# SSM preparation of a hybrid backbone: exponents by 34-row one-pass products plus a mask product, an exponential per direction, nothing computed on POOL

## The chip, the cores and the metric

One core of one Trainium2 chip runs the whole program. The metric is the device time of one execution in microseconds (us), the median of several runs. Engines: PE (TensorE; PEld are its weight loads), DVE (VectorE), ACT (ScalarE), POOL (GpSimd), SP (SyncE). A letter q behind an engine (SPq, POOLq) means its queue: what it issues or waits for.

## The reference, cut to what matters

Two layers of a backbone with three token mixers. The third is a bidirectional Mamba-2 state-space scan (SSD) over chunks of tokens. The preparation computes, for every tile of 128 tokens and each of 16 heads, the part of the output that stays inside the tile. Per direction:

```
acum  = cumsum(a)                                    # a = dt * A, the log decay, per token and head
lmat  = exp(where(lower, acum[l] - acum[s], -inf))   # 128 x 128 per head; the mirror image for backward
cb    = C[l] . B[s]                                  # 128 x 128 per group of 8 heads
y     = (cb * lmat) @ (x * dt)                       # 64 channels per head
out   = y_forward + y_backward + ssm_d * x
```

There are 1024 sample tokens and 128 prompt tokens, so 9 tiles per layer (NT = 9), 16 heads (SH), 64 channels per head (SP_), 2 groups (SG).

## The kernel before

Each layer is a sequence of phases with a barrier of all five engines between them. After the projections (phase 1) comes the decay phase (phase 2): DVE and ACT compute dt and the log decay `logd` of all tiles, PE sums them to `cum` (running sums, times triangles of ones) and `tot`, and a few rows are turned and stored in DRAM (`cumrow_d`, `betarow_d`, L691 and L692) before the barrier. Then comes the stage in question, the SSM preparation (phase 3), followed by the SSM scan.

The preparation treats the 9 tiles one after another; tile t is double buffered by p = t % 2. For a tile:

- SP loads `xin` (12 blocks of 128x128, L698), and later stores the turned tokens `xt` (L702).
- PE turns 10 blocks (L1003) into PSUM banks 0 to 2 and makes the two group products `cb` in bank 7 (L1005). Then it makes the exponents of all 16 heads in banks 3 to 6: for each head one f32 product of `after` with a triangle of ones (forward, L1014) and one of `before` with the other triangle (backward, L1015), added in PSUM. Last it makes the 32 output products of the **previous** tile (two per head: L990 with `w_f`, L991 with `w_b`), 64 columns each, into banks 0 and 1.
- ACT copies the turned tile to `xt` (L1443) and takes the exponential in two halves of 8 heads (`e_ssm`, L1450).
- DVE masks `cb` by both triangles (L1991), builds `after` for the next tile (L1980: a strict triangle times the log decay, in two halves), adds the output products of the previous tile to `d_x` (`y_sum`, L1984, one instruction of 1024 elements), makes `x_dt[0]` (L2000), `d_x` (L2001) and `w_f` (L2004, two halves).
- POOL builds `before` (L1676), `x_dt[1]` (L1688) and `w_b` (L1692) in the same way.

PE's next turning (L1003 of tile t + 1) writes the banks that the output products of tile t - 1 were in, so it waits for `y_sum(t - 1)`:

```
if not (isinstance(t, int) and t < 2):
    pe.wait_ge(sp_yd, n - 1)
```

After the last tile PE waits for `y_sum(7)` and makes the output products of tile 8. The tiles 0, 1 and 8 are written out, 2 to 7 are a loop.

Of the kernel before, what the change touches and what calls it, by code (L numbers as in the profile page):

```python
# [24 lines left out]
ALU = mybir.AluOpType  # L25
# [5 lines left out]
P = 128  # L31
# [86 lines left out]
def backbone_kernel(nc, A, O, table, rope_table):  # L118
    with ExitStack() as ctx:
# [13 lines left out]
        ssm_tok_d = dram("ssm_tok_d", [NT, P, 1280])  # L133

# [56 lines left out]
        plus_half = fixed("plus_half", [P, GH])  # L191
        r_tok = fixed("r_tok", [P, NT])
# [37 lines left out]
        after = place(a, "after", [P, SH, P])  # L230
        before = place(a, "before", [P, SH, P])
        e_ssm = place(a, "e_ssm", [P, SH, P])
        w_f = place(a, "w_f", [P, SH, P])
        a2 = fresh(WT)
        w_b = place(a2, "w_b", [P, SH, P])
        x_dt = [place(a2, f"x_dt{n}", [P, SH, SP_]) for n in range(2)]
        d_x = place(a2, "d_x", [P, SH, SP_])
        cb = [place(a2, f"cb{n}", [P, 2, SG, P]) for n in range(2)]
# [108 lines left out]
        rest = place(a, "rest", [P, 2, NT, 20])  # L347
        cum_g = place(a, "cum_g", [P, NT, 2, GH])
# [53 lines left out]
        sp_prod = sem("sp_prod")  # L402
        sp_fwd = sem("sp_fwd")
        sp_bwd = sem("sp_bwd")
        sp_e = sem("sp_e")
        sp_yd = sem("sp_yd")
        sp_y = sem("sp_y")
# [242 lines left out]
        def _(sp):  # L650
# [14 lines left out]
            with sp.Fori(0, DEPTH) as l:  # L665
# [24 lines left out]
                sp.wait_ge(row_made, l + 1)  # L690
# [212 lines left out]
        def _(pe):  # L903
# [21 lines left out]
            with pe.Fori(0, DEPTH) as l:  # L925
# [53 lines left out]
                last.then_inc(decay_prod, 1)  # L979
                barrier(pe, l, 2)  # L980


                def y_products(n, late):

                    for half in range(2):
                        pe.wait_ge(sp_fwd, n * 6 + (5 + late + half))
                        pe.wait_ge(sp_bwd, n * 4 + (3 + late + half))
                        for h in range(8 * half, 8 * half + 8):
                            dst = PSUM[:, h * SP_:(h + 1) * SP_]
                            pe.matmul(dst, w_f[:, h], x_dt[0][:, h], start=True, stop=False)  # L990
                            last = pe.matmul(dst, w_b[:, h], x_dt[1][:, h], start=False, stop=True)  # L991
                    last.then_inc(sp_y, 1)

                def ssm_prep(t, p, i):
                    n = l * NT + t
                    first = isinstance(t, int) and t == 0
                    pe.wait_ge(tile_in[p], loaded(l, p, i, 0))
                    if not first:
                        pe.wait_ge(sp_fwd, n * 6 - 2)
                    if not (isinstance(t, int) and t < 2):  # L1000
                        pe.wait_ge(sp_yd, n - 1)
                    for k in range(10):
                        pe.transpose(PSUM[:, k * P:(k + 1) * P], xin[p][:, k], ident)  # L1003
# [3 lines left out]
                    for half in range(2):  # L1007
                        if not first:
                            pe.wait_ge(sp_e, n * 2 + (half - 1))
                        pe.wait_ge(sp_fwd, n * 6 + (1 if first else -1) + half)  # L1010
                        pe.wait_ge(sp_bwd, n * 4 + (1 if first else -1) + half)
                        for h in range(8 * half, 8 * half + 8):
                            dst = PSUM[:, 1536 + h * P:1536 + (h + 1) * P]
                            pe.matmul(dst, after[:, h], cst[:, C_TRI], start=True, stop=False)  # L1014
                            last = pe.matmul(dst, before[:, h], cst[:, C_TRI + 1], start=False, stop=True)  # L1015
                        last.then_inc(sp_prod, 1)
# [1350 lines left out]
```

## Time and profile before

| what | value |
|---|---|
| median of 3 runs | 5475.16 us (5473.5 to 5489.51) |
| the profiled execution: its own time / its span | 5479.28 us / 5477.5 us |
| granted TensorE clock, mean of the span | 0.865 of full |
| PE / PEld busy | 4459.5 us (81%) / 4161.0 us (76%) |
| DVE / ACT / POOL busy | 2261.2 us (41%) / 932.3 us (17%) / 798.0 us (15%) |
| SSM preparation, layer 1 | 1091.40 to 1284.59 us of the span (193.2 us) |
| SSM preparation, layer 2 | 3786.40 to 3980.26 us (193.9 us) |

The busy shares are of the whole program. The preparation is two stretches of about 193 us in it, and only these and the short decay phases ahead of them are changed. A granted clock of 1.00 is 2.4 GHz, one of 0.50 is 1.2 GHz.

### The profile page before, as it was taken

How to read it: one execution, taken by the hardware profiler on the slowest of the kernel's cores; microseconds unless marked ns; L12 is line 12 of the kernel's file. 1: busy time of each engine (PE TensorE's matmuls, PEld its weight loads, DVE VectorE, ACT ScalarE, POOL GpSimd, SP SyncE). 2: the span in 40 equal slices, each digit the busy share in tenths (PEclk: the TensorE clock that was granted, in tenths of full speed). 3: DMA queues.
4: the chain of work that ended last, by engine and by line, in shares of the span. 5: the costliest groups of instructions: out<-in, count | busy, mean ns of one | idle time of the engine just before them, and what ended most of it. 6: DMA issues, size and time to landing. Idle time of an engine off the chain costs nothing.

```text
span 5477.5 us, 67948 instructions
## 1 busy us (share of the span) xinstructions
PE 4459.5 (81%) x26457; PEld 4161.0 (76%) x26457; DVE 2261.2 (41%) x2622; ACT 932.3 (17%) x1477; POOL 798.0 (15%) x668
## 2 busy tenths in 40 slices
PE   5899999787794775798759999996878828649977
PEld 2899999784783665788739999996848728648867
DVE  2532511277425245544235143114863243464442
ACT  2111100010211220342021011001111112114410
POOL 0010000077110002100000000002660100030000
PEclk7999999898785777899879999997988658769988
DMA  6222222123234332001242222221142434310024
GB/s 207 96 88 78 89 95 86 48 85 116 84 108 157 113 104 78 8 8 59 96 165 86 83 82 94 94 78 55 63 142 77 141 121 126 100 51 7 8 76 149
DMA packets 418307, 492.97 MB, mean 90 GB/s; under 512 B 83102, under 2 KB 354512, under 8 KB 410612
## 3 DMA queue, kind: packets, MB, share of 16 engines
q1 hardware_dynamic: 385160, 392.54, 22.9%
q0 software_dynamic: 28240, 96.75, 4.6%
q8 instruction: 134, 2.20, 0.2%
q10 hardware_dynamic: 4700, 0.88, 0.1%
q14 instruction: 73, 0.60, 0.0%
HBM read 333.19 MB, written 156.91 MB: 89 GB/s over the span
## 4 chain that ended last, share of the span: by engine, by line
PE 70%; DVE 9%; DMA 8%; issue 4%; SPq 3%; POOL 2%; ACT 2%; DVEq 1%; POOLq 0%; ACTq 0%
PE PSUM L633 14%; PE PSUM L634 14%; PE PSUM L635 14%; PE PSUM L1271 5%; PE PSUM L1118 4%; PE PSUM L1292 3%; PE PSUM L991 1%; PE PSUM L990 1%; DMA g_XY<-xy_d 1%; PE PSUM L1260 1%; DMA w_mod<-in_w_mod 1%; SPq L823 1%; POOL x_in L1710 1%; PE PSUM L1261 1%; PE PSUM L1096 1%
## 5 line engine op out<-in xcount | busy, mean ns | idle before, releaser
L633 PE MATMUL PSUM<-h_hi,w_hi 128*128 128x384 f32 x3456 | 1156.5, 335 | 40.6 <-DVE w_lo L619 40.6
L635 PE MATMUL PSUM<-h_hi,w_lo 128*128 128x384 f32 x3456 | 1156.0, 334 | 0.0
L634 PE MATMUL PSUM<-h_lo,w_hi 128*128 128x384 f32 x3456 | 1156.0, 334 | 0.0
L633 PEld LDWEIGHTS PSUM<-h_hi,w_hi 128*128 128x128 f32 x3456 | 650.1, 188 | 40.7 <-issue 40.7
L634 PEld LDWEIGHTS PSUM<-h_lo,w_hi 128*128 128x128 f32 x3456 | 650.1, 188 | 0.0
L635 PEld LDWEIGHTS PSUM<-h_hi,w_lo 128*128 128x128 f32 x3456 | 649.9, 188 | 0.0
L633 PE MATMUL PSUM<-b_hi,w_hi 128*128 128x384 f32 x1152 | 394.6, 343 | 108.5 <-DVE w_lo L619 56.4
L617 DVE CAST w_hi<-w_raw 128x2048 fp32r<-128x2048 f32 (+1 forms) x104 | 118.9, 1144 | 789.1 <-PE PSUM L635 587.1
L634 PE MATMUL PSUM<-b_lo,w_hi 128*128 128x384 f32 x1152 | 391.9, 340 | 0.0
L635 PE MATMUL PSUM<-b_hi,w_lo 128*128 128x384 f32 x1152 | 391.4, 340 | 0.0
L1658 POOL DMA_DIRECT2D proj_d<-leave x140 | 82.5, 589 | 1744.7 <-ACT leave L1411 669.4
L633 PEld LDWEIGHTS PSUM<-b_hi,w_hi 128*128 128x128 f32 x1152 | 221.9, 193 | 113.9 <-issue 107.7
L2285 DVE TENSOR_REDUCE row_max<-PSUM 128x1 f32<-128x1152 f32 (+1 forms) x144 | 178.3, 1238 | 252.0 <-PE PSUM L1261 252.0
L1271 PE MATMUL PSUM<-v_all,prob_t 128*128 128x64 f32 x2336 | 278.1, 274 | 0.1
L1271 PEld LDWEIGHTS PSUM<-v_all,prob_t 128*128 128x128 f32 x2336 | 275.2, 194 | 0.5 <-DVE prob_t L2296 0.5
L1118 PE MATMUL PSUM<-g_XY,g_t 128*128 128x128 f32 x288 | 59.9, 393 | 251.2 <-DMA g_XY<-xy_d 243.7
L1118 PEld LDWEIGHTS PSUM<-g_XY,g_t 128*128 128x128 f32 x288 | 55.1, 293 | 254.2 <-DMA g_XY<-xy_d 202.4
L619 DVE TENSOR_TENSOR w_lo<-w_raw,w_hi 128x2048 fp32r<-128x2048 f32 (+1 forms) x104 | 221.3, 2128 | 7.9
L634 PEld LDWEIGHTS PSUM<-b_lo,w_hi 128*128 128x128 f32 x1152 | 222.1, 193 | 0.0
L635 PEld LDWEIGHTS PSUM<-b_hi,w_lo 128*128 128x128 f32 x1152 | 221.6, 192 | 0.0
L1411 ACT ACTIVATE leave<-PSUM 128x1152 f32<-128x1152 f32 x60 | 68.1, 1135 | 680.7 <-PE PSUM L635 680.7
L1292 PE MATMUL PSUM<-cst,prob 128*128 128x128 f32 x1168 | 157.9, 278 | 25.5 <-ACT prob L1598 25.4
(294 smaller groups left out, 7010.7 us busy)
## 6 DMA issues: line engine op xcount, KB each, us to landing
w_raw<-in_w_in SPq DMA_DIRECT2D x70, 1024.0 KB, 5.2
proj_d<-leave POOLq DMA_DIRECT2D x140, 512.0 KB, 2.9
g_t<-gdn_tile_d SPq DMA_DIRECT2D x36, 1024.0 KB, 8.6
gdn_tile_d<-g_out SPq DMA_DIRECT2D x18, 1792.0 KB, 7.0
wide<-proj_d SPq DMA_DIRECT2D x48, 576.0 KB, 3.8
w_mod<-in_w_mod SPq DMA_DIRECT2D x12, 2048.0 KB, 18.8
xs<-ssm_tok_d SPq DMA_DIRECT2D x36, 640.0 KB, 5.0
qk_t<-proj_d SPq DMA_DIRECT2D x36, 512.0 KB, 9.6
```

Of the source, the lines that this page charges most:

```text
L617: dve.tensor_copy(w_hi[p][:, 0:kt], w_raw[p][:, 0:kt])
L619: dve.tensor_tensor(w_lo[p][:, 0:kt], w_raw[p][:, 0:kt], w_hi[p][:, 0:kt].bitcast(F32), ALU.subtract).then_inc(w_ready[p], 1)
L633: pe.matmul(dst, wh, x_hi[:, k, lo:hi], start=(k == 0), stop=False)
L634: pe.matmul(dst, wh, x_lo[:, k, lo:hi], start=False, stop=False)
L635: last = pe.matmul(dst, wl, x_hi[:, k, lo:hi], start=False, stop=(k == kt - 1))
L823: sp.dma_start(gd[d]["XY"][t % 2][at, :, at], src.rearrange("h x (j i) -> j h x i", i=SOLVE)).then_inc(scan_in[d][t % 2], 16)
L1118: last = pe.matmul(bank(n, P, h * P), lhs(h), rhs(h), start=True, stop=True)
L1271: last = pe.matmul(bank(7, AD, h * AD), prob_t[s][:, j], v_all[:, kt, g * AD:(g + 1) * AD], start=(j == 0), stop=(j == len(key_tiles) - 1))
L1292: last = pe.transpose(dst, prob[s][:, j * P:(j + 1) * P], ident)
L1411: act.activation(thirds(leave[b][:, 0:T]), acc(b), f, scale=sc).then_inc(leave_ready[b], 1)
L1658: pool.dma_start(proj_d[j * 2 + (blk + b), :, 0:SAMPLE], leave[b][:, 0:SAMPLE]).then_inc(leave_out[b], 16)
L2285: dve.tensor_reduce(row_max[:, u, h:h + 1], PSUM[:, 1536 * (h % 2):1536 * (h % 2) + nk * P], AX_X, ALU.max, negate=True).then_inc(at_m, 1)
```

## The change

The exponents are no longer sums over triangles. The running sums `cum` exist already; the exponent of (s, l) is their difference. Each is split into a coarse part (rounded to fp32r, the one-pass format) and the rest (`ssm_hl`), turned by PE in the decay phase, and stored in DRAM as `ssmrow_d`. Per tile and direction POOL's queue loads 32 rows (`s_col`) and two long rows (`s_row[32:34]`) from there. One product over 34 rows, 4 heads wide (512 columns), gives the differences; a second one, the identity times a constant of 0 and -1e30 (`far_r`), adds the mask. The directions are now separate: own exponent products, own exponential, own weights `w_ssm[d]`. The output products stay as they are (32 f32 products of 64 columns), but are made in two groups of 8 heads, with the exponents of the second direction between them, and `y_sum` is done by halves. `d_x` moves from DVE to ACT as 16 activations of 64 columns, `x_dt[1]` and the backward weights move from POOL to DVE, `after` and `before` are gone, `cb` is copied unmasked. `x_dt` and `d_x` are double buffered. The loops over tiles are written out.

```
@@ tiles in SBUF
-        after = place(a, "after", [P, SH, P])
-        before = place(a, "before", [P, SH, P])
+        e_ssm = [place(a, f"e_ssm{d}", [P, SH, P]) for d in range(2)]
+        w_ssm = [place(a, f"w_ssm{d}", [P, SH, P]) for d in range(2)]
+        s_row = [place(a2, f"s_row{d}", [34, SH, P], F32R) for d in range(2)]
+        s_col = [place(a2, f"s_col{d}", [34, P], F32R) for d in range(2)]
+        x_dt = [[place(a2, f"x_dt{n}{d}", [P, SH, SP_]) for d in range(2)] for n in range(2)]
@@ decay phase: SP, PE, ACT, POOL, DVE
-                sp.wait_ge(row_out, l * 32 + 32)
+                sp.wait_ge(row_made, l * 2 + 2)
+                sp.dma_start(flat_rows[0:512].rearrange("(c p) n -> p c n", p=P), ssm_rows[:, 0:4].bitcast(F32)).then_inc(row_out, 16)
+                sp.dma_start(flat_rows[512:576], ssm_rows[0:64, 4].bitcast(F32)).then_inc(row_out, 16)
+                sp.wait_ge(row_out, l * 64 + 64)
+                for c in range(5):
+                    last = pe.transpose(bank(6, P, c * P)[0:width] if c < 4 else bank(7, P)[0:width], ssm_cols[:, c * P:c * P + width], ident)
+                act.activation(ssm_rows[:, 0:4], bank(6).rearrange("p (c n) -> p c n", n=P), ACT.Copy)
+                act.activation(ssm_rows[0:64, 4], bank(7, P)[0:64], ACT.Copy).then_inc(row_made, 1)
+                pool.tensor_tensor(head_of[:], ident[0:32, 0:SH], ident[0:32, SH:32], ALU.add)
+                for d in range(2):
+                    pool.tensor_scalar(s_row[d][0:32], over(head_of[:], P), -1.0, None, ALU.mult)
+                    pool.tensor_copy(s_col[d][32:34], ones[32:34])
+                    dve.tensor_copy(ssm_hl[:, :, d, 0], cum[:, d, :, 4:20])
+                dve.drain()
+                    dve.tensor_tensor(ssm_hl[:, :, d, 1], cum[:, d, :, 4:20], ssm_hl[:, :, d, 0].bitcast(F32), ALU.subtract)
@@ PE, preparation
+                def y_products(t, half):
+                    pe.wait_ge(sp_w, n * 4 + 2 + 2 * half)
+                    for h in range(8 * half, 8 * half + 8):
+                        pe.matmul(dst, w_ssm[0][:, h], x_dt[p][0][:, h], start=True, stop=False)
+                        last = pe.matmul(dst, w_ssm[1][:, h], x_dt[p][1][:, h], start=False, stop=True)
+                def exponents(t, d):
+                    if d == 0:
+                        for e in range(2):
+                            pe.wait_ge(s_in[e], (n + 1) * 32)
+                    for half in range(2):
+                        if t or d:
+                            pe.wait_ge(sp_e, n * 4 + 2 * d + half - 1)
+                        for c in range(2):
+                            pe.matmul(dst.rearrange("p (h t) -> p h t", t=P), ident_r[:], again(far_r[:, d], 4), start=True, stop=False)
+                            last = pe.matmul(dst, s_col[d][:], s_row[d][:, hs].rearrange("k h t -> k (h t)"), start=False, stop=True)
+                        last.then_inc(sp_d, 1)
+                for t in range(NT):
...
+                    exponents(t, 0)
+                    pe.wait_ge(out_ready, n + 1)
+                    if t:
+                        y_products(t - 1, 0)
+                    exponents(t, 1)
+                    if t:
+                        y_products(t - 1, 1)
@@ ACT, per tile: xt copy, then
+                    for d in range(2):
+                        for half in range(2):
+                            act.wait_ge(sp_d, n * 4 + 2 * d + half + 1)
+                            if t:
+                                act.wait_ge(sp_w, n * 4 - 3 + 2 * half + d)
+                            act.activation(e_ssm[d][:, hs], src, ACT.Exp).then_inc(sp_e, 1)
+                    for h in range(SH):
+                        last = act.activation(d_x[p][:, h], xt[p][:, h * SP_:(h + 1) * SP_], ACT.Copy, scale=rows[:, 80 + h:81 + h])
@@ POOL, preparation: only loads
+                for t in range(NT):
+                    for d in range(2):
+                        if t:
+                            pool.wait_ge(sp_d, (l * NT + t) * 4 - 2 + 2 * d)
+                        pool.dma_start(s_row[d][32:34].rearrange("s h n -> s (h n)"), ssmrow_d[t, d].rearrange("(s h) n -> s (h n)", s=2)).then_inc(s_in[d], 16)
+                        pool.dma_start(s_col[d][0:32], ssmrow_d[t, d]).then_inc(s_in[d], 16)
@@ DVE, per tile
+                    dve.tensor_copy(cb[p][:], bank(7, 256).rearrange("p (g l) -> p g l", l=P)).then_inc(sp_cb, 1)
+                    for d in range(2):
+                        dve.tensor_tensor(x_dt[p][d][:], xt[p][:, 0:D_MODEL].rearrange("p (h q) -> p h q", q=SP_), over(dt_[:, t, d], SP_), ALU.mult)
+                    for half in range(2):
+                        if t:
+                            y_sum(t - 1, half)
+                        for d in range(2):
+                            dve.wait_ge(sp_e, n * 4 + 2 * d + half + 1)
+                            dve.tensor_tensor(w_ssm[d][:, hs], e_ssm[d][:, hs], again(cb[p][:, half], 8), ALU.mult).then_inc(sp_w, 1)
```

## Rows read from the trace of the kernel before

**Rows 1.** The page: the chain that ended last, by line

```profile
PE PSUM L633 14%; PE PSUM L634 14%; PE PSUM L635 14%; PE PSUM L1271 5%; PE PSUM L1118 4%; PE PSUM L1292 3%; PE PSUM L991 1%; PE PSUM L990 1%; DMA g_XY<-xy_d 1%; PE PSUM L1260 1%; DMA w_mod<-in_w_mod 1%; SPq L823 1%; POOL x_in L1710 1%; PE PSUM L1261 1%; PE PSUM L1096 1%
```

**Rows 2.** SP's queue in order of time: starts of the scan, the preparation, the scan

```profile
1284.59 1.03 SPq L724 DMA_DIRECT2D s_io<-in_state_ssm  x2
...
3786.40 1.18 SPq L698 DMA_DIRECT2D xin<-proj_d  x2
...
3980.26 1.03 SPq L724 DMA_DIRECT2D s_io<-in_state_ssm  x2
```

**Rows 3.** Chain in order of time, layer 1: start us, us, what

```profile
1091.40 5.21 DMA xin<-proj_d
1096.66 2.40 PE PSUM L1003 x10
1099.06 0.85 PE PSUM L1005 x4
...
1134.20 1.24 DVE y_acc L1984
...
1172.04 1.31 PE PSUM L1003 x10
...
1259.41 1.22 DVE y_acc L1984
```

**Rows 4.** Stretches of the preparation, layer 1: two steady tiles, two parts of the tail

```profile
core 0: us, PE busy (x) PEld busy (x) DVE busy (x) ACT busy (x) POOL busy (x), PEclk, DMA share, GB/s
...
1170.75:1188.18 17.43, 16.00 (x142) 15.86 (x142) 15.86 (x9) 3.29 (x3) 13.51 (x5) 1.00 0.26 83
1188.18:1207.24 19.06, 17.63 (x142) 17.50 (x142) 15.28 (x10) 3.28 (x3) 14.29 (x5) 0.91 0.24 76
...
1259.40:1269.00 9.60, 0.00 (x0) 0.00 (x0) 9.42 (x5) 0.00 (x0) 8.46 (x3) 0.63 0.00 0
1269.00:1283.20 14.20, 13.91 (x64) 13.73 (x64) 1.26 (x2) 0.00 (x0) 0.00 (x0) 0.50 0.00 1
```

**Rows 5.** Order of time on PE: first exponent product, first output product of a tile

```profile
1173.63 0.39 PE L1014 MATMUL PSUM<-cst,after 128*128 128x128 f32 x2
...
1180.78 0.33 PE L990 MATMUL PSUM<-x_dt,w_f 128*128 128x64 f32 x2
```

**Rows 6.** Order of time on PE in the attention: one-pass products of 512 columns

```profile
2242.48 0.39 PE L1260 MATMUL PSUM<-k_hi,q_now 128*128 128x512 f32 x1
2242.71 0.39 PE L1261 MATMUL PSUM<-k_lo,q_now 128*128 128x512 f32 x1
```

**Rows 7.** A line on DVE: duration ns min/median/max

```profile
L2004 DVE TENSOR_TENSOR w_f<-e_ssm,cb x36: 1211/3358/3376, 1117.6 to 3964.6; 128x1024 f32<-128x1024 f32 x36
```

**Rows 8.** Order of time on ACT: four scaled copies in a row

```profile
1587.61 1.14 ACT L1493 ACTIVATE g_out<-PSUM,norm_k 128x128 f32<-128x128 f32 x4 [2.70 <-POOL norm_k L1743]
```

**Rows 9.** Loads: a line of POOL's queue with its landing; a group of SP's queue

```profile
L1659 POOL DMA_DIRECT2D proj_d<-leave x140: 538/542/550, 176.6 to 3750.6; - x140
...
DMA to landing us min/median/max: 1.8/2.7/4.7
...
g_t<-gdn_tile_d SPq DMA_DIRECT2D x36, 1024.0 KB, 8.6
```

**Rows 10.** Short stretches of layer 1, columns as in rows 4

```profile
1125.00:1130.00 5.00, 5.00 (x25) 5.00 (x25) 4.89 (x2) 0.72 (x1) 3.81 (x2) 0.50 0.01 2
...
1138.00:1140.00 2.00, 2.00 (x15) 2.00 (x15) 2.00 (x1) 1.13 (x1) 2.00 (x2) 0.74 0.00 0
...
1190.00:1192.00 2.00, 2.00 (x13) 2.00 (x11) 2.00 (x2) 0.00 (x0) 2.00 (x2) 0.56 0.00 0
```

**Rows 11.** Decay phase in order of time; POOL's one-input pass over 1024 elements

```profile
1086.89 0.53 DVE L1969 TENSOR_TENSOR rest<-tot,cum 128x360 f32<-128x360 f32 x1
...
1089.60 0.35 SPq L692 DMA_DIRECT2D betarow_d<-row_sb  x1
...
L1786 POOL CAST q_now<-q_stack 128x1024 fp32r<-128x1024 f32 x6 | 6.1, 1039 | 92.3 <-PE PSUM L1261 72.9 <-DVEq L495 19.4
```

More of the change, by code:

```diff
@@ L979, in _ @@
                 last.then_inc(decay_prod, 1)
-                barrier(pe, l, 2)
-                def y_products(n, late):
-                    for half in range(2):
[L986 to L1003, printed above, removed]
+                ssm_cols = ssm_hl[:].rearrange("p t d s h -> p (t d s h)").bitcast(F32)
@@ L1006, in ssm_prep @@
                     last.then_inc(transposed, 1)
[L1007 to L1016, printed above, removed]
-                    pe.wait_ge(out_ready, nth(l, t, 0, 1) + 1)
-                    if not first:
-                        y_products(n - 1, 2)
-                ssm_prep(0, 0, 0)
-                ssm_prep(1, 1, 0)
-                with pe.Fori(0, 3) as i:
-                    for p in range(2):
-                        ssm_prep(i * 2 + (p + 2), p, i + 1)
-                ssm_prep(NT - 1, 0, 4)
-                pe.wait_ge(sp_yd, l * NT + NT - 1)
-                y_products(l * NT + NT - 1, 0)
+                    exponents(t, 0)
[5 more added lines that the diff above has]
+                        y_products(t - 1, 1)
+                pe.wait_ge(sp_yd, (l * NT + NT - 1) * 2)
+                for half in range(2):
+                    y_products(NT - 1, half)
                 barrier(pe, l, 3)
@@ L1974, in _, with y_sum @@
                 barrier(dve, l, 2)
-                def build_after(t):
+                def y_sum(t, half):
+                    dve.wait_ge(sp_y, (l * NT + t) * 2 + 1 + half)
+                    cols_ = slice(512 * half, 512 * half + 512)
+                    dve.tensor_tensor(y_acc[:, t, cols_], PSUM[:, cols_], d_x[t % 2][:].rearrange("p h q -> p (h q)")[:, cols_], ALU.add).then_inc(sp_yd, 1)
+                for t in range(NT):
+                    n, p = l * NT + t, t % 2
+                    dve.wait_ge(transposed, nth(l, t, 0, 5) + 1)
+                    dve.tensor_copy(cb[p][:], bank(7, 256).rearrange("p (g l) -> p g l", l=P)).then_inc(sp_cb, 1)
+                    dve.wait_ge(out_ready, n + 1)
+                    for d in range(2):
+                        dve.tensor_tensor(x_dt[p][d][:], xt[p][:, 0:D_MODEL].rearrange("p (h q) -> p h q", q=SP_), over(dt_[:, t, d], SP_), ALU.mult)
+                    dve.drain()
+                    dve.wait_ge(sp_dx, n)
@@ L2013, in _ @@
+                dve.wait_ge(sp_dx, l * NT + NT)
+                for half in range(2):
+                    y_sum(NT - 1, half)
                 barrier(dve, l, 3)
```

138 lines of the change are left out of this document (50 added, 88 removed).

## The prediction

> **What bounds the kernel now.** I read the page's chain first: the projection products lead it (L633 to L635, 14% each) [rows 1], and the change does not touch them. What can move is the two preparation stretches and the decay phase ahead of each. SP's queue and the chain show their ends: in layer 1 from the first `xin` load at 1091.40 [rows 3] to the first load of the scan at 1284.59, in layer 2 from 3786.40 to 3980.26 [rows 2]. That is 193.2 and 193.9 us, 387.1 in all, 7% of the span. Then I followed layer 1 in order of time [rows 3] and cut it in three, always at the start of a `y_sum` (L1984). The **head** runs to the first one, 1134.20: 42.8 us. The **steady part** is the seven turns from there to `y_sum(7)` at 1259.41: 125.2 us, 17.9 each. The **tail** is the rest: 25.2 us.
>
> In a steady tile PE is busy 16.00 of 17.43 us, DVE 15.86, POOL 13.51, ACT 3.29 [rows 4]. PE starts turning at 1172.04 [rows 3], the exponents at 1173.63, the output products at 1180.78 [rows 5]. So turning and group products take 1.59 us and the 32 exponent products 7.15, 0.2233 each. If the 32 output products cost the same although they have half the columns, 17.43 leaves 1.54 us, in which PE waits for `y_sum` (1.24 us [rows 3]) and the wake-ups around it. PE's 16.00 busy us say the same: 1.6 + 7.15 + 7.15. PE bounds the steady part.
>
> DVE is close behind, but not by its own work: `w_f` takes 1.21 us at best and 3.36 at the median, one and the same instruction [rows 7], and the short ones are those beside which POOL computes nothing. The tail shows the price: for 9.60 us PE does nothing while DVE and POOL finish tile 8's weights (9.42 and 8.46 us busy), then it makes 32 output products in 14.2 us at a granted clock of 0.50 [rows 4].
>
> **The change, part by part.** *Exponents.* Removed: 32 products, 7.15 us per tile. Added: 16 one-pass products of 512 columns. Two such products of the attention start 0.23 us apart [rows 6], so 16 cost 3.70 us. No row shows a 34-row operand or a repeated one; the nearest row is this one, and I take 0.23 for both kinds. Lower bound 0.20, if fewer rows save a little; upper bound 0.43, the same at the lower clock (0.23 by 13.9 / 7.15, what output products cost at either clock).
>
> *Output products* stay: 7.15 us. *The turn:* only the last half of `y_sum` stands behind the last product, 0.65 us instead of 1.24 (half the elements), so 1.54 becomes 0.97. *Turning* stays: 1.59. The steady cycle is 1.59 + 3.70 + 7.15 + 0.97 = **13.4 us** for 17.43.
>
> *Would another engine bound it?* DVE with POOL quiet, by the short end of [rows 7]: four weights and two `x_dt` at 1.21, two half sums at 0.65, a small copy of 0.4: 9.0 us of 13.4. ACT: one copy and two exponentials made 3.29 us for 3328 elements [rows 4], about 1.0 per 1024, so now 5.3 us. To that come 16 scaled copies of 64 columns. Four of 128 columns take 1.14 us, so start some 0.26 apart [rows 8]; for 64 I take 0.2 each, 3.3 us, upper bound 0.26 or 4.2. ACT's last exponential can only follow the second exponents, which end 8.9 us into the cycle (1.59 + 1.85 + 3.57 + 1.85). Exponential and copies end at 8.9 + 1.1 + 3.3 = 13.3; the next `xt` copy is due at 13.4 + 1.6 = 15.0. It fits, by 1.7 us.
>
> *The row loads.* POOL issues two loads when PE is through with a direction, 0.54 us each, landing 1.8 to 4.7 us later, median 2.7 [rows 9]. The second direction's are issued from 8.9, the last lands at 8.9 + 0.1 + 0.6 + 2.7 = 12.3 (bounds 11.4 and 14.3). PE wants it at 15.0. Hidden, by 0.7 us even at the slow end. The cover is half the output products, the turn and the turning (6.1 us); in tile 1 no output products stand ahead, so there the wait shows.
>
> *Head.* `xin` lands 5.3 us in; turning and group products at the lower clock 3.3 (2.40 + 0.85 [rows 3]), to 8.6. Exponents of tile 0, half of them at the lower clock, to 11.3; the second direction follows ACT's exponentials, to 13.4. Turning of tile 1 to 15.0; its rows are issued from 13.4 and land at 16.9, a wait of 1.9. Then 1.85, 3.57, 1.85 and 3.57 for exponents and output products: `y_sum(0)` starts at 27.9 instead of 42.8.
>
> *Tail.* `y_sum(7)` 0.65 and wake-up 0.3, 7.15 for 32 output products whose weights are ready by then, the last half sum and the barrier 1.1: 9.2 us for 25.2.
>
> *Sum.* 27.9 + 7 x 13.4 + 9.2 = 131 us per layer if the clock is full from tile 0 on. It will not quite be: two of the seven steady tiles took 19.06 instead of 17.43 [rows 4], with a clock of 0.56 while PE turned them [rows 10]. I add the same 3.3 us, and for the tail half of the 7.15 that the lower clock would cost, 3.5. That makes 138 us per layer, 276 for 387.1: **111 us less**.
>
> How the clock comes back matters more than any term. From 1125 to 1130 PE is busy 5.00 of 5.00 us with output products and the clock stays at 0.50; at 1138 to 1140, with tile 2's turnings and exponents, it is at 0.74 on its way up [rows 10]. In the tail it stays at 0.50 for 14 us of output products [rows 4]. So output products hold a clock but do not raise it. The Trainium skill (TensorE: Matmul & The Clock Gate, Part 1) says that sustained matmul activity releases the throttle. By that no tail could stay low and the result would be 7 us lower; the trace contradicts it for these products.
>
> *Decay phase.* Ahead of `rest` come two small copies, a drain and two subtractions, about 1 us by `rest`'s own 0.53 for 360 elements [rows 11]. Behind it five more turnings at the lower clock, 1.2 us (ten take 2.40 [rows 3]), ACT's copies, 0.7, and two stores of 288 KB together, somewhat longer than those issued at 1089.60 [rows 11]: 3 us in all less what ran beside them. POOL's set-up of 2 x 2048 elements at 1.04 us per 1024 [rows 11] is 4 to 5 us; it is beside DVE's first steps and may hold them up by 0 to 2, I take 1. Per layer 4 us, both 8 (bounds 5 and 16). The mask and identity copies at the start are covered by the token loads: nothing.
>
> Net 111 - 8 = 103. The profiled execution took 5479.28 us, its span 5477.5, both some 3 above the median of 5475.16; a difference carries over, so **5475 - 103 = 5372 us**. Own range: 131 per layer and 5 of decay give 5355; 150 per layer (a low clock in a few more places) and 13 give 5401.
>
> **Rivals.** *The rows come late.* Loads on a full queue landed after 8.6 us [rows 9], and `xin` and `xt` traffic runs in the same stretch. With 8.6 the rows come at 18.2 for 15.0: 3.2 us for each of 8 tiles in 2 layers, 51 us: 5423. Against it: these are small loads, and the longest landing on POOL's queue was 4.7.
>
> *POOL's issues wait for DVE.* If each of the two waits for a DVE instruction of 1.2 us, the last row comes 2.4 later, at 14.7, still in time; with the landing at its slow end at 16.7, 1.7 us late: 27 us, 5399. Against it: the issues took 538 to 550 ns in all 140 cases [rows 9], beside a DVE that splits weights. The Trainium skill (SBUF — State Buffer, Who interferes with whom) states this rule: descriptors of a load issued from GpSimd starve while VectorE holds the shared port. These issues show none of it.
>
> *ACT sets the cycle*, if a scaled copy costs more than that [rows 8]: 0.37 us makes 5.9, past 15.0 by 0.9 a tile: 14 us, 5386. Less gain, not none.
>
> *The clock stays low*, the other side. At 0.50 a cycle is 3.25 + 16 x 0.43 + 32 x 0.4267 + 1.0 = 24.8 us and the layer some 229, so 2 x 229 + 8 - 387 = +79: 5554. It decides from about 60% of the stretch at the lower clock: (189.5 - 131) / 98. For it: output products grow from 41% to 53% of the cycle and do not raise the clock, and no row shows whether 34-row products do. Against: every tile keeps 5.3 us of turnings and exponents, and PE's idle turn shrinks from 1.54 to 0.97.
>
> **How the numbers follow.** Own case 0.75, rows late 0.10, issues wait 0.04, ACT 0.05, clock low 0.06. From 5352 to 5428 the range holds the first four and their mixtures. 0.3% is 16 us, about what a measurement of this kernel can tell from no change. All but the clock case are faster by more; of that one, milder forms end near or a little below before: faster 0.93, same 0.02, slower 0.05.
>
> **What would show it.** Steady tiles of 13.4 us at a clock of 1.00; exponent products 0.23 apart; every DVE product at 1.2; POOL with issues only; PE waiting for rows in tile 1 alone; a tail of 9 us, or 16 at the lower clock. Wrong would be a wait of PE for `s_row` or `s_col` in each tile, a clock near 0.5 through the output products, or DVE waiting for ACT's `d_x`.

## The result and the profile after

The changed kernel takes 5638.1 us (median of 4 runs, 5619.15 to 5647.44) beside 5474.54 us before (4 runs): ratio 1.0293, 95% interval 1.0266 to 1.0319. It is 2.9% slower; the forecast was 1.9% faster, and 5428 the upper end of its range. The profiled execution took 5619.15 us with a span of 5617.5, so it is the shortest of the four. The shares below are read from it, and it stands 139.9 us above the profiled one of before.

SP's queue gives the stages, as in [rows 2], the kernel's line numbers having moved (start us, us):

```profile
1096.31 1.17 SPq L709 DMA_DIRECT2D xin<-proj_d  x2
...
1346.08 1.03 SPq L735 DMA_DIRECT2D s_io<-in_state_ssm  x2
3862.96 1.20 SPq L709 DMA_DIRECT2D xin<-proj_d  x2
...
4115.02 1.02 SPq L735 DMA_DIRECT2D s_io<-in_state_ssm  x2
```

The two preparation stretches last 249.8 and 252.1 us, together 501.8 where they had been 387.1: +114.7. The decay phase, read as in the forecast from the copy that opens it to the first `xin` load, is 37.15 us for 28.3 per layer: +17.7 in both. That makes 132.4 of the 140.0 by which the spans differ. The other 7.6 lie in code that the change does not touch: one stretch of layer 2's attention (4965.53 to 5241.42 before) alone takes 283.9 us for 275.9, with the same number of PE records, at a granted clock of 0.94 for 0.96.

The page's chain by line, which answers to [rows 1]:

```profile
PE PSUM L640 14%; PE PSUM L641 14%; PE PSUM L642 14%; PE PSUM L1287 5%; PE PSUM L1134 3%; PE PSUM L1308 3%; PE PSUM L1005 2%; PE PSUM L1006 2%; PE PSUM L1021 2%; PE PSUM L1020 1%; PE PSUM L1276 1%; DMA g_XY<-xy_d 1%; PE PSUM L1277 1%; SPq L834 1%; DMA w_mod<-in_w_mod 1%
```

The output products (L1005, L1006) have gone from 1% to 2% each, and the exponents (L1020, L1021), on no line of it before, hold 3%. Two steady tiles, the tail's products and a longer stretch of layer 1, in the columns of [rows 4]:

```profile
core 0: us, PE busy (x) PEld busy (x) DVE busy (x) ACT busy (x) POOL busy (x), PEclk, DMA share, GB/s
1168.40:1195.20 26.80, 25.97 (x95) 20.04 (x95) 8.89 (x10) 9.14 (x21) 2.03 (x4) 0.56 0.18 57
1195.20:1224.30 29.10, 28.32 (x94) 21.13 (x94) 8.74 (x10) 9.15 (x21) 2.03 (x4) 0.50 0.16 53
1331.00:1346.00 15.00, 13.92 (x64) 13.73 (x64) 3.74 (x5) 0.00 (x0) 0.00 (x0) 0.50 0.00 0
1140.00:1200.00 60.00, 57.64 (x210) 44.60 (x209) 21.19 (x23) 19.53 (x43) 4.06 (x8) 0.56 0.16 51
```

A tile takes 26.8 or, once in layer 1, 29.1 us instead of 17.4, and PE is busy for all but 0.8 of them. No other engine is near: DVE 8.9, ACT 9.1, POOL 2.0. Besides the 0.8 us for the last half of `y_sum`, PE waits for nothing in a steady tile; it has fewer instructions (95 records for 142) and needs more time for them, at a granted clock of 0.50 to 0.56 (1.2 GHz, with short stays at 2.4) where it had been 1.00. PE in order of time in the first of these tiles shows two things at once:

```profile
1168.44 2.40 PE L1029 MATMUL PSUM<-cst,xin 128*128 128x128 f32 x10 [0.78 <-DVE y_acc L1991]
1170.63 1.06 PE L1032 MATMUL PSUM<-xin 128*128 128x128 f32 x4
...
1173.53 0.50 PE L1020 MATMUL PSUM<-far_r,ident_r 128*128 128x512 f32 x1
1173.96 0.50 PE L1021 MATMUL PSUM<-s_row,s_col 34*128 34x512 f32 x1
1174.39 0.51 PE L1020 MATMUL PSUM<-far_r,ident_r 128*128 128x512 f32 x1
...
1176.42 0.63 PE L1005 MATMUL PSUM<-x_dt,w_ssm 128*128 128x64 f32 x2
...
1182.94 0.79 PE L1020 MATMUL PSUM<-far_r,ident_r 128*128 128x512 f32 x1
1183.66 0.79 PE L1021 MATMUL PSUM<-s_row,s_col 34*128 34x512 f32 x1
1184.39 0.79 PE L1020 MATMUL PSUM<-far_r,ident_r 128*128 128x512 f32 x1
```

First the spacing. Two one-pass products of 512 columns started 0.23 us apart in the attention [rows 6]; these start 0.43 apart at full clock, and 0.72 at the low one in the tile's second half. Second the clock. It comes up among the first exponents and is gone before the first eight heads' output products are through, although the forecast had these hold a clock. Short stretches, columns as above:

```profile
1172.60:1175.20 2.60, 2.60 (x7) 1.10 (x6) 2.12 (x2) 1.47 (x2) 0.00 (x0) 1.00 0.45 187
...
1176.40:1181.00 4.60, 4.60 (x24) 4.60 (x23) 0.00 (x0) 0.06 (x1) 0.50 (x2) 0.50 0.68 183
1181.50:1187.00 5.50, 5.50 (x10) 2.28 (x9) 3.05 (x3) 1.02 (x1) 0.00 (x0) 0.50 0.00 0
```

In 2.60 us at full clock PE makes 7 products and counts as busy throughout, with weight loads for only 1.10 of it; in the steady tile of [rows 4] they were busy for 15.86 of 17.43. Soon after, the clock is at 0.50, with PE never idle in the record.

The weights, copies and row loads are as forecast. Lines of DVE and POOL (duration ns min/median/max):

```profile
L2008 DVE TENSOR_TENSOR w_ssm<-e_ssm,cb x72: 1214/1219/1227, 1108.4 to 4101.1; 128x1024 f32<-128x1024 f32 x72
...
L1704 POOL DMA_DIRECT2D s_row<-ssmrow_d x36: 507/507/592, 1096.7 to 4066.1; - x36
...
L1705 POOL DMA_DIRECT2D s_col<-ssmrow_d x36: 502/519/545, 1097.3 to 4066.6; - x36
```

Groups of POOL's loads (KB each, median us to landing), and ACT in order of time:

```profile
s_row<-ssmrow_d POOLq DMA_DIRECT2D x36, 16.0 KB, 2.1
s_col<-ssmrow_d POOLq DMA_DIRECT2D x36, 16.0 KB, 2.1
```

```profile
1188.31 3.91 ACT L1474 ACTIVATE d_x<-xt,rows 128x64 f32<-128x64 f32 x16
```

All 72 weight products are at the short end of [rows 7], and no issue on POOL waited for one of them.

The decay phase in order of time, POOL and DVE:

```profile
1057.63 5.39 POOL L1694 TENSOR_SCALAR s_row<-head_of 32x2048 fp32r<-32x2048 f32 x1 [0.24 <-issue]
...
1059.93 3.33 DVE L1935 TENSOR_SCALAR dec_neg<-dec_pre 128x432 f32<-128x432 f32 x1
...
1063.46 5.39 POOL L1694 TENSOR_SCALAR s_row<-head_of 32x2048 fp32r<-32x2048 f32 x1
1063.71 3.87 DVE L1938 TENSOR_TENSOR dec_neg<-dec_neg,dec_pre 128x432 f32<-128x432 f32 x1
```

POOL's set-up is 5.39 us a direction, and two DVE steps of 432 elements last 3.33 and 3.87 us. The first ends at 1063.26, 0.24 us after POOL's first pass; the second lies within POOL's second pass.

### The profile page after: what moved, and what is told of

Read it like the earlier page. It is cut to its first block, busy times and chain, and to the rows that moved or that the text cites. A ratio compares the mean times of both kernels' runs of the same rounds, so it can differ in the third digit from the quotient of the medians.

```text
span 5617.5 us, 66426 instructions
## 1 busy us (share of the span) xinstructions
PE 4615.2 (82%) x25603; PEld 4212.1 (75%) x25603; DVE 2144.5 (38%) x2630; ACT 1039.2 (18%) x1805; POOL 606.4 (11%) x662
## 4 chain that ended last, share of the span: by engine, by line
PE 72%; DVE 8%; DMA 8%; issue 4%; SPq 3%; POOL 2%; ACT 1%; DVEq 1%; POOLq 0%; ACTq 0%
PE PSUM L640 14%; PE PSUM L641 14%; PE PSUM L642 14%; PE PSUM L1287 5%; PE PSUM L1134 3%; PE PSUM L1308 3%; PE PSUM L1005 2%; PE PSUM L1006 2%; PE PSUM L1021 2%; PE PSUM L1020 1%; PE PSUM L1276 1%; DMA g_XY<-xy_d 1%; PE PSUM L1277 1%; SPq L834 1%; DMA w_mod<-in_w_mod 1%
## 5 line engine op out<-in xcount | busy, mean ns | idle before, releaser
L1287 PE MATMUL PSUM<-v_all,prob_t 128*128 128x64 f32 x2336 | 283.9, 277 | 0.1
```

What stands on the lines that cost most here:

```text
L1287: last = pe.matmul(bank(7, AD, h * AD), prob_t[s][:, j], v_all[:, kt, g * AD:(g + 1) * AD], start=(j == 0), stop=(j == len(key_tiles) - 1))
```

## The experiments

The open question was why the clock does not hold, and what the 0.43 is. The first theory was that the exponent products over 34 rows are the cause of both. Rivals were a stall between products of different row counts (with the clock only following it) and the new order of the exponents and output products. "Stage" is the sum of the two preparation stretches of the profiled execution; clock is the granted one in its window from 1140 to 1200, so in layer 1 alone; apart is start to start at full clock. All kernels but the first are the changed one with the edit named. The kernel before was run again beside each group of them (medians 5475 to 5485 us), and the ratios are to those runs.

| kernel | exponent products | us | ratio to before (95%) | stage | clock | apart |
|---|---|---|---|---|---|---|
| before | f32 sums over triangles | 5474.54 | 1 | 387.1 | 0.97 | none of this form |
| changed | mask 128 rows, difference 34 | 5638.1 | 1.0293 (1.0266 to 1.0319) | 501.8 | 0.56 | 0.43 |
| e4 | same, order as before | 5646.85 | 1.0307 (1.0287 to 1.0328) | 500.7 | 0.56 | 0.43 |
| e3 | same, grouped in twos | 5459.63 | 0.9975 (0.9962 to 0.9987) | 327.8 | 0.98 | 0.33 mean |
| e2 | 34 and 34 | 5579.73 | 1.0187 (1.016 to 1.0215) | 445.6 | 0.53 | 0.23 |
| e5 | 128 and 64 | 5551.76 | 1.0145 (1.0118 to 1.0172) | 435.5 | 0.78 | 0.42 |
| e12 | 64 and 64 | 5462.48 | 0.9956 (0.9934 to 0.9978) | 334.9 | 0.79 | 0.23 |
| e11 | 128 and 66 | 5421.84 | 0.9887 (0.9857 to 0.9917) | 302.2 | 1.00 | 0.23 |
| e10 | 128 and 96 | 5416.31 | 0.9871 (0.9837 to 0.9905) | 275.8 | 1.00 | 0.23 |
| e1 | 128 and 128 | 5417.12 | 0.9886 (0.9863 to 0.9909) | 286.5 | 0.99 | 0.23 |

### All rows (e1)

Both operands of the difference product get 128 rows; the rows from 34 on multiply by zero.

```
-        s_row = [place(a2, f"s_row{d}", [34, SH, P], F32R) for d in range(2)]
-        s_col = [place(a2, f"s_col{d}", [34, P], F32R) for d in range(2)]
+        s_row = [place(a2, f"s_row{d}", [P, SH, P], F32R) for d in range(2)]
+        s_col = [place(a2, f"s_col{d}", [P, P], F32R) for d in range(2)]
...
-                pool.tensor_tensor(head_of[:], ident[0:32, 0:SH], ident[0:32, SH:32], ALU.add)
+                pool.tensor_tensor(head_of[:], ident[:, 0:SH], ident[:, SH:32], ALU.add)
...
```

> The second product of each exponent pair is padded with zero rows to all 128 rows (the result is the same). Theory A (rows): in the changed kernel the change between a 34-row and a 128-row operand is what spaces the products 0.72 us at the lower clock and 0.42 at the full one, and products over 34 rows do not hold the clock up. Then the spacing falls to 0.23 us, the clock is near 1.00 in the preparation, a steady tile takes 13.4 instead of 26.8 us, and the time is 5619 - 2 x 9 x 13 = about 5385 us. Theory B (order: the dense block of a tile is cut in two and output products have a larger share, rows do not matter): spacing and clock stay, time unchanged within 20 us. Theory C (the spacing comes from the rows, the clock from the order): spacing 0.43 at the lower clock, tile 26.8 - 16 x 0.25 = 22.8 us, about 5550 us.

Measured: 5417.12 us, 221 less than the changed kernel, 1.1% below the one before, and 32 above what the first theory gave. A window over one and a half tiles, and two exponent products:

```profile
1160.00:1180.00 20.00, 19.22 (x143) 17.89 (x142) 13.12 (x15) 11.88 (x24) 3.05 (x6) 1.00 0.35 113
```

```profile
1160.80 0.39 PE L1020 MATMUL PSUM<-far_r,ident_r 128*128 128x512 f32 x1
1161.03 0.39 PE L1021 MATMUL PSUM<-s_row,s_col 128*128 128x512 f32 x1
...
1172.08 1.31 PE L1029 MATMUL PSUM<-cst,xin 128*128 128x128 f32 x10 [0.78 <-DVE y_acc L1991]
...
1185.41 1.31 PE L1029 MATMUL PSUM<-cst,xin 128*128 128x128 f32 x10 [0.78 <-DVE y_acc L1991]
```

The products start 0.23 us apart, the clock is full, and a tile takes 1185.41 - 1172.08 = 13.33 us. The output products are the same share of the work as in the changed kernel, so their share is not what kept the clock down there. Rows of zeros bring both effects down together, so this run doesn't yet say which is which.

### No change of rows (e2)

The mask product uses 34 of its 128 rows, and the exponential takes 0 times its input. So this kernel leaves the decay and the mask out of the output; its PE, ACT and DVE instructions stay as many and as large.

```
-                            pe.matmul(dst.rearrange("p (h t) -> p h t", t=P), ident_r[:], again(far_r[:, d], 4), start=True, stop=False)
+                            pe.matmul(dst.rearrange("p (h t) -> p h t", t=P), ident_r[0:34], again(far_r[0:34, d], 4), start=True, stop=False)
...
-                            act.activation(e_ssm[d][:, hs], src, ACT.Exp).then_inc(sp_e, 1)
+                            act.activation(e_ssm[d][:, hs], src, ACT.Exp, scale=0.0).then_inc(sp_e, 1)
```

> Both products of a pair work on 34 rows; the mask then covers only 34 of 128 rows, and the exponential is taken of 0 times its input, so that the decay is left out of the output. Theory A: no change of row count any more, so the spacing is 0.43 us at the lower clock (0.23 at full), but the clock stays low, since now even fewer rows work: a steady tile takes 3.3 + 16 x 0.43 + 32 x 0.427 + 1 = 24.8 us, about 5585 us. Theory B: spacing unchanged at 0.72 (not caused by rows), 5630 us. If the clock only asks for time without gaps, it comes up and a tile takes 13.4 us: 5385 us.

Measured: 5579.73 us. PE in order of time at full clock, and a long window:

```profile
1166.09 0.39 PE L1020 MATMUL PSUM<-far_r,ident_r 34*128 34x512 f32 x1
1166.32 0.39 PE L1021 MATMUL PSUM<-s_row,s_col 34*128 34x512 f32 x1
```

```profile
1140.00:1200.00 60.00, 58.43 (x232) 51.39 (x232) 21.34 (x23) 21.36 (x45) 5.08 (x10) 0.53 0.24 76
```

The spacing is back at 0.23, so a 34-row product is no slower than any other; what costs is the step from one row count to the other. That is worth 501.8 - 445.6 = 56 us, at a clock that is the same over the whole stage (0.54 for 0.55). But the clock stays at 0.53, with no such step between the exponents and PE busy 58.43 of 60 us. The stalls are not what keeps it down here.

### Fewer changes (e3)

Per half, both mask products first and then both difference products: half as many changes, same products.

```
                         for c in range(2):
-                            hs = slice(8 * half + 4 * c, 8 * half + 4 * c + 4)
                             dst = bank(3 + 2 * half + c)
                             pe.matmul(dst.rearrange("p (h t) -> p h t", t=P), ident_r[:], again(far_r[:, d], 4), start=True, stop=False)
+                        for c in range(2):
+                            hs = slice(8 * half + 4 * c, 8 * half + 4 * c + 4)
+                            dst = bank(3 + 2 * half + c)
                             last = pe.matmul(dst, s_col[d][:], s_row[d][:, hs].rearrange("k h t -> k (h t)"), start=False, stop=True)
```

> Per half the two mask products come first, then the two 34-row products: half as many changes between row counts, same work. Theory A: of four starts two are 0.72 and two 0.43 us apart at the lower clock, so 16 x 0.145 = 2.3 us less per tile, 42 us less in all, unless the clock comes up too. Theory B (another cause of the spacing, as an operand that repeats): no change.

Measured: 5459.63 us, and a surprise for my theory: with the same 34 rows the clock came up and stayed.

```profile
1140.00:1200.00 60.00, 56.86 (x373) 44.72 (x372) 33.91 (x36) 36.17 (x84) 8.11 (x16) 0.98 0.32 102
```

```profile
1185.39 0.71 PE L1019 MATMUL PSUM<-far_r,ident_r 128*128 128x512 f32 x2
1186.03 0.73 PE L1023 MATMUL PSUM<-s_row,s_col 34*128 34x512 f32 x2
```

Two products now take 0.65 us instead of 0.86. The weight loads don't decide about the clock either: they are busy 44.72 of the 60 us here and 44.60 in the changed kernel. So neither the rows alone nor the stalls alone decide about the clock: 34 rows in all products kept it down without a stall, and 34 rows in half of them left it up once half of the stalls were gone. It is a small reordering, and it is worth 178 us against the changed kernel, though against the one before only 0.25%.

### The old order (e4)

```
                     exponents(t, 0)
                     pe.wait_ge(out_ready, n + 1)
-                    if t:
-                        y_products(t - 1, 0)
                     exponents(t, 1)
                     if t:
+                        y_products(t - 1, 0)
                         y_products(t - 1, 1)
```

> Only the order of PE's work is as it was: exponents of both directions, then all 32 output products of the previous tile. Theory A: the clock stays low, since the rows are the same; PE waits besides for ACT between the two directions (about 1 us a tile), so 0 to 20 us slower than the changed kernel. Theory B: the dense block is whole again, the clock comes up to near 1.00 and a tile takes 16 us or less: 5430 us.

Measured: 5646.85 us, stage 500.7, clock 0.56: no difference. The order in which exponents and output products alternate is not the cause.

### 64 rows (e5)

As e1, but the products read 64 rows (`s_col[d][0:64]`, `s_row[d][0:64, hs]`).

> As the run with 128 rows, but the second product is padded with zero rows only to 64. If any change of row count is what spaces the products, they stay 0.42 us apart at the full clock and 0.72 at the lower one; if what counts is a mismatch with the 34 alone (not a power-of-two part of the array), they fall to 0.23. Theory A on the clock (rows times time at work): with 64 rows there is more work than with 34 at the same spacing; between the changed kernel (5619 to 5647) and the run with 128 rows (5417). With the spacing kept and the clock up a tile takes 13.3 + 16 x 0.19 = 16.4 us, about 5475; with the clock still low about 5635.

Measured: 5551.76 us.

```profile
1165.17 0.49 PE L1021 MATMUL PSUM<-s_row,s_col 64*128 64x512 f32 x1
1165.59 0.49 PE L1020 MATMUL PSUM<-far_r,ident_r 128*128 128x512 f32 x1
```

```profile
1140.00:1220.00 80.00, 76.86 (x369) 58.14 (x368) 35.08 (x36) 33.30 (x72) 7.99 (x16) 0.78 0.24 76
```

The products still start 0.42 apart and not 0.23, as with 34 rows (0.43), while the clock is between those of the changed kernel and e1. Only rows of zeros in the difference products (and their set-up ahead of the stage) differ from the changed kernel. The 0.78 is no steady state, though: in layer 2 the clock over the same part of the stretch (3855 to 3915) is 0.53, and its stretch lasts 230.2 us beside 205.3 in layer 1. In the changed kernel it is 252.1 and 249.8, so 64 rows gain in both layers, and unequally.

### Where the step begins (e10, e11, e12)

Is it any change of the row count, or a border between 64 rows and more? e10 and e11 read 96 and 66 rows, e12 reads 64 in both products (mask `ident_r[0:64]`, `far_r[0:64, d]`, and the scale of 0 as in e2, so it too leaves out the decay and the mask).

> The difference products go over 96 rows (62 of them zeros) beside mask products over 128. Theory A, a mode of the array: products of at most 64 rows run in another division of the array than those of 128, and only a change between the two makes PE finish the one before the next begins. 96 rows count as 128 then: the products start 0.23 us apart at full clock, a steady tile takes 13.3 us and the time is that of the kernel with 128 rows, 5400 to 5430. Theory B, any change of the row count: starts 0.42 apart as with 34 and 64 rows, a steady tile of 16.5 us even at full clock, and 5417 + 16 tiles x 3.1 = 5467 or more.

> The difference products go over 66 rows (32 of them zeros), two more than the run with 64 rows that gave 5552 and a clock of 0.78. Theory A: starts 0.23 apart; what two rows more change is then the mode alone. Theory B: 0.42 apart and 5540 to 5555, as two rows more change nothing. For the clock: if it follows the number of rows by itself, it stays near 0.78 in the stretch from 1140 to 1220 and the time ends at 5480 to 5530; if it follows the mode or the stalls between the products, it is at 1.00 and the time at 5400 to 5430.

> Mask products and difference products both over 64 rows; the mask product then covers 64 of 128 positions and the exponential has a factor of 0, so the decay and the mask are left out of the output. No change of rows within the exponents: starts 0.23 apart at full clock by either theory. What it tells is the clock, beside the run with both over 34 rows (5580, clock 0.53 from 1140 to 1200). If the number of rows counts, 64 rows bring the clock up to 0.7 or more and the time to 5430 to 5530; if it is the mode that counts, it stays near 0.53 and the time near 5580.

Measured: 5416.31, 5421.84 and 5462.48 us. PE in order of time with 66 rows:

```profile
1155.20 0.40 PE L1020 MATMUL PSUM<-far_r,ident_r 128*128 128x512 f32 x1
1155.44 0.40 PE L1021 MATMUL PSUM<-s_row,s_col 66*128 66x512 f32 x1
1155.67 0.40 PE L1020 MATMUL PSUM<-far_r,ident_r 128*128 128x512 f32 x1
```

and its window, then that of e12:

```profile
1140.00:1200.00 60.00, 56.86 (x428) 53.21 (x427) 37.85 (x39) 39.18 (x95) 9.15 (x18) 1.00 0.38 117
```

```profile
1140.00:1200.00 60.00, 57.65 (x327) 50.38 (x326) 30.03 (x31) 29.31 (x66) 7.10 (x14) 0.79 0.30 95
```

Between 64 rows and 66 the step vanishes (0.42 to 0.23), and the time falls by 130 us. Any-change theory B is dead; the border is what counts. The Trainium skill has a rule that would fit (TensorEngine Tiling (Array Packing), Tiling Modes): the array can be run divided in tiles of 128, 64 or 32 rows, and a change of that mode drains the engine. These runs agree, with 0.42 for 0.23 us between products of up to 64 rows and of 128; that section does not say that a product of few rows takes such a mode by itself, which the step from 64 to 66 rows suggests and no run here shows.

For the clock, e2 and e12 differ in rows alone, both without a step within the exponents: 34 rows 0.53 and stage 445.6, 64 rows 0.79 and 334.9. So the number of rows counts by itself, 111 us of stage here. In e12's mask products the 30 more rows hold the identity and the mask and are not zeros; that rows of zeros count is shown by e5.

Three kernels with stages of 275.8, 286.5 and 302.2 us (e10, e1, e11) have medians within 6 us. In the profiled executions the reason lies again in layer 2's attention, which is the same code in all: the stretch of 275.9 us before takes 292.8 at a clock of 0.91 in e10 and e1, and 275.4 at 0.96 in e11. Why it wanders is open. So differences of under about 17 us between whole kernels don't tell what the preparation does; the stage does.

### Versions on top of 128 rows (e6 to e9)

e6 takes the set-up from POOL: `head_of` is made once at the kernel's start, and ACT writes the constants ahead of the decay phase.

```
+                for d in range(2):
+                    act.activation(s_row[d][:], over(head_of[:], P), ACT.Copy, scale=-1.0)
+                    act.activation(s_col[d][:], ones, ACT.Copy)
...
-                for d in range(2):
-                    pool.tensor_scalar(s_row[d][:], over(head_of[:], P), -1.0, None, ALU.mult)
-                    pool.tensor_copy(s_col[d][:], ones)
```

> 128 rows, and the constant rows of s_row are made by ACT at the start of the decay phase instead of by POOL. Theory: POOL's two passes of 5.39 us hold up DVE's first steps there (one of 0.39 took 3.33, one of 0.61 took 3.87), 6 us per layer; on ACT they lie beside those steps. So DVE's steps are at 0.39 and 0.61 again and the time is 2 x 6 = 12 us below the run with 128 rows, about 5405. Rival: DVE's steps were slow for another reason, or ACT's own passes (about 1.8 us each) come in the way of its first exponential: no gain or up to 4 us lost.

Measured: 5408.56 us (ratio 0.987, 0.9852 to 0.9888). The decay phase falls from 37.17 to 30.83 us per layer, and the two DVE steps are back at their own length:

```profile
1061.22 0.39 DVE L1934 TENSOR_SCALAR dec_neg<-dec_pre 128x432 f32<-128x432 f32 x1
...
1061.97 0.61 DVE L1937 TENSOR_TENSOR dec_neg<-dec_neg,dec_pre 128x432 f32<-128x432 f32 x1
...
1110.17 0.79 PE L1020 MATMUL PSUM<-far_r,ident_r 128*128 128x512 f32 x1 [3.57 <-DMA s_col<-ssmrow_d]
```

3.33 - 0.39 and 3.87 - 0.61 make 6.2 us, all of the 6.3 that the phase gave back. The Trainium skill (SBUF — State Buffer, Who interferes with whom) has a rule for this: VectorE and GpSimd share a pair of ports, and whoever issues first holds it for the whole instruction. The first step agrees with it; the second ends 1.27 us before POOL's pass is recorded to end, and spans on POOL are rough. The last line above is the wait that the forecast had placed in tile 1: PE waits 3.57 us for the rows.

e7 shortens it: each direction waits for its own rows (`pe.wait_ge(s_in[d], (n + 1) * 32)` in place of a wait for both).

> As the run with 128 rows and ACT's set-up, but PE waits before the exponents of a direction only for the rows of that direction (the changed kernel waits for both before the first). Theory: in tile 1 PE stood still 3.6 us for the second direction's rows, and after that its clock was at 0.50 for some 12 us of exponents and output products. Both go: 3.6 + about 5 us per layer, 17 in all: about 5391 us. Rival: the wait only moves to the second direction, and the clock drops all the same: within 5 us of 5408.

Measured: 5399.17 us (0.9852, 0.9837 to 0.9868), stage 281.3 for 288.3. The wait only became another: PE now waits for ACT's `xt` copy, 2.63 us in layer 1 and 2.49 in layer 2, and the clock after it, to the next turning, is 0.66 where it had been 0.65. That turning starts 34.8 and 34.0 us into the stretch instead of 36.5 and 36.8, which is 4.5 us gained in all. Over the whole stretch layer 1 gained nothing (144.0 in both kernels) and layer 2 gained 7.1, for the clock dips in two later tiles of layer 1 (in one in e6) and stays higher in the tail of layer 2. The interval overlaps that of e6, so the gain stands in the stage alone.

e8 is e7 with the backward weights on POOL again.

```
-                        for d in range(2):
-                            dve.wait_ge(sp_e, n * 4 + 2 * d + half + 1)
-                            dve.tensor_tensor(w_ssm[d][:, hs], e_ssm[d][:, hs], again(cb[p][:, half], 8), ALU.mult).then_inc(sp_w, 1)
+                        dve.wait_ge(sp_e, n * 4 + half + 1)
+                        dve.tensor_tensor(w_ssm[0][:, hs], e_ssm[0][:, hs], again(cb[p][:, half], 8), ALU.mult).then_inc(sp_w[0], 1)
...
+                        pool.tensor_tensor(w_ssm[1][:, hs], e_ssm[1][:, hs], again(cb[p][:, half], 8), ALU.mult).then_inc(sp_w[1], 1)
```

> As the run before it, but the backward weights are made by POOL again, between its row loads; all else stays. Theory (the part 'nothing computed on POOL' is worth little once PE is at 13.3 us a tile): DVE's products beside POOL's go from 1.2 to 2 to 3.4 us, but both engines stay under 13.3 us, so steady tiles stay at 13.3 and only the tail is longer, 5 us per layer: about 5401. Rival: the held-up products make the weights or the row loads late in each tile: 2 us or more a tile, 5430 or more.

Measured: 5388.56 us (0.9846, 0.9832 to 0.9861), the lowest median of all, but the same as e7 within the intervals. Its stage is 284.2 us, 2.9 more than e7's; the attention of layer 2 is 13.7 us shorter in its profile. DVE's weights now take 2.08 us on the average instead of 1.2, and the steady tile is still 13.35 us: PE bounds it, and DVE's longer products cost nothing there. That POOL computes nothing, a part of the change, is worth 3 us at most at this pace, by the stage.

e9 is e7 with the exponents of both directions ahead of all output products.

> As the first run of this call, but exponents of both directions come before all 32 output products, as in the kernel before. Theory: with 128 rows the clock holds in either order; PE waits for ACT's exponentials of the first direction between the two, 2 x 1.0 us less what the products cover, about 1 us a tile, 16 us in all: about 5407. Rival: the split order is what keeps the clock up, so here it dips once a tile, 1.6 us each: 5420 or more.

Measured: 5419.26 us (0.9891, 0.9875 to 0.9907), near the rival's 5420. The trace decides for the theory: turnings start at 1159.31 and 1173.40, so a tile takes 14.09 us at full clock, 0.76 more than 13.33, and PE stands still for about 0.45 us in it until ACT's exponential is through. With rows over 64 the split order is worth that, 12 of the 18.6 us by which the stage is longer than e7's (299.9 for 281.3). In steady tiles the clock doesn't depend on it; in layer 1 it came up later (0.70 for 0.89 from 1125 to 1140), which one trace can't ascribe.

## Why the prediction was wrong, point by point

**What bounds the kernel** was right: PE bounds the steady tile, and DVE's long weights went with POOL's arithmetic. Neither was where the time went.

**The step that failed is the term of the exponents**, "I take 0.23 for both kinds". The forecast said itself that no row shows a 34-row operand. Its upper bound, 0.43, was meant for the low clock; at full clock the products really start 0.43 apart and at the low one 0.72, outside the bounds. Per tile that is 3.2 or 4.6 us, and by e2 56 us in the stage. The larger part is the clock: the sum took it as full but for a few places, and the stage of 501.8 us lies 226 above the forecast's 276, 170 of them still there in e2, which has no steps between exponents. Both go when the rows do (e1, e10, e11).

**The rival "the clock stays low" is what happened**, and it had a chance of 0.06. Of its two grounds one held: 34-row products did not keep the clock up. The other, the larger share of output products, does not bring the clock down by itself, since e1, e10 and e11 have the same share and a clock of 0.99 to 1.00. Its price needs two additions: 5554, plus the 56 us of the late starts, which a sum with 0.43 at the low clock didn't hold, plus 10 for the decay phase, gives 5620, beside 5619.15 in the profiled execution. That it meets to the microsecond is luck: by this sum the stage would be 514 us, 12 more than measured, and the attention's 8 us are not in it. By tile: 24.8 plus 16 times 0.29 is 29.4, and the window shows 29.10. The median of the four runs is 19 us higher, which no profile explains.

**The argument against that rival was wrong.** "Every tile keeps 5.3 us of turnings and exponents" counted 34-row exponents as work that raises the clock. The clock does come up among them, in the first direction, but falls with PE busy all the time, and it falls among output products, of which the forecast had read in [rows 10] that they hold a clock. What brings it back is shown in steps: in part 64 rows instead of 34 (e2 to e12), and almost wholly either 66 rows for 64, where the late starts go (e5 to e11), or half as many changes (e3). The forecast saw that no row showed how 34-row products act, and gave the case 6 in 100 all the same. An operand form of which the trace has no row, in half of the exponent products, and a clock that [rows 4] show fragile deserved far more than that.

**With more than 64 rows the forecast of the tile holds**, and the gain in the whole is about half of the forecast one: a tile of 13.33 us for 13.4; stage 275.8 to 302.2 for 276, the excess in e11 where the clock came up later (0.63 from 1125 to 1140, 1.00 in e10); 5416 to 5422 us for 5372. Of those 45 us, 10 are the decay phase and 10 to 26 the stage in e1 and e11, and in e10 none; 17 in e1 and e10 are the stretch of layer 2's attention at its lower clock. The rest was not traced.

**DVE, ACT, row loads:** weights at 1.22 us, loads hidden with a landing of 2.1 us. Sixteen scaled copies take 3.91 us (forecast 3.3, bound 4.2) and PE waits for none of them. The two rivals about late rows and POOL's issues did not come up. The wait of PE in tile 1, forecast at 1.9 us, is at most 0.2 us in the changed kernel; it appeared where the exponents ran faster (4.61 and 3.91 us in e1, 3.57 in e6).

**The decay phase** was mis-sized: 8.9 us per layer for 4, just past the bound of 16 for both. POOL's pass costs 5.39 us per direction and not the 2.1 taken from a 1024-element row of another form [rows 11]; of the "0 to 2" that it might hold up DVE it made 6.2. The rest, 2.7, stands beside the 3 forecast for the small subtractions, the turnings and the stores.

## What to carry to other kernels

Do not alternate products of up to 64 rows with products of 128: pad the short ones with zero rows past 64, which cost no time per product of 512 columns here, or else put those of a kind side by side. When a change takes work off a TensorE-bound stage, ask of each new product whether the trace holds one of the same rows and columns; where it doesn't, the granted clock is the first thing to doubt, and a stage whose clock dips already can lose more than all the work removed. A pass on GpSimd set beside VectorE has to be priced by what it holds up, not by its own length.

## What the runs showed of the hardware

- Between one-pass products of 512 columns, a step between 128 rows and 34 or 64, either way, makes the next one start 0.19 to 0.20 us later at full clock and 0.29 at the low one; between 128 rows and 66 or 96 it costs nothing.
- A granted clock of 0.50 can go with a PE that is never idle: 5.50 of 5.50 us busy in the changed kernel. In e2 it is 58.43 of 60 at 0.53.
- Rows count for the clock, zeros too: both products over 34 rows 0.53, over 64 rows 0.79 (e2, e12); beside 128-row masks 34 rows give 0.56, 64 rows with 30 of zeros 0.78 in layer 1 and 0.53 in layer 2 (e5), and 66 rows or more 0.99 to 1.00. The same 34 rows beside 128-row masks give 0.56 with a change at every product and 0.98 with a change at every second (e3). What decides about it stays open: the rows and the steps between them both move it, and no run here reduces the two to one.
- Even with 128 rows the clock is not firm: in e7 it dips in two later tiles of layer 1 and one of layer 2, whose turnings take 2.3 to 2.4 us for 1.31. The same stretch of layer 2's attention takes 275 to 293 us in different kernels, at 0.96 to 0.90.
- One POOL pass of 32 x 2048 elements with an fp32r output from a repeated input takes 5.39 us, and made DVE steps of 0.39 and 0.61 us last 3.33 and 3.87.
